# Four copies of local key and value caches, issued in the down projection by ScalarE and not in the first projections by SyncE

## The reference, cut to what matters

```
mod = silu(c) @ w_ada + b_ada                 # 6 x 1024 columns: shift, scale, gate, twice
h = x * (1 + scale1) + shift1
proj = h @ w_in                               # 1024 x 3072: qa, ka, va, qb, kb, vb, 512 columns each
... rotary, dilated window attention (A), paged differential attention (B)
mixed = concat(oa, ob) @ w_o
x = layer_norm(ALPHA * x + gate1 * mixed)
u = (x * (1 + scale2) + shift2) @ w_up        # 1024 x 5632
y = (gelu(conv(a)) * conv(g)) @ w_down        # 2816 x 1024
x = layer_norm(ALPHA * x + gate2 * y)
kk = concat([cwk, k], 1); vv = concat([cwv, v], 1)
win_k_sample, win_v_sample = kk[:, DS:], vv[:, DS:]
```

## Time and profile before

| | us |
|---|---|
| median of 3 runs | 1179.2 (1174.07 to 1181.84) |
| the profiled execution | 1176.66 |
| its span, first to last instruction | 1175.0 |
| PE busy | 1023.7 (87%) |
| DVE busy | 827.1 (70%) |
| POOL busy | 450.5 (38%) |
| ACT busy | 270.8 (23%) |

### The profile page before, as it was taken

One profiled execution on the slowest core, in us unless ns is written; L12 is line 12 of the kernel. 1 busy time (PEld: TensorE's weight loads), 2 busy tenths in 40 slices (PEclk: granted clock), 3 DMA queues, 4 the chain that ended last, 5 costly groups with the idle time before them and its releaser, 6 DMA issues.

```text
span 1175.0 us, 23900 instructions
## 1 busy us (share of the span) xinstructions
PE 1023.7 (87%) x9297; PEld 832.1 (71%) x9297; DVE 827.1 (70%) x1545; ACT 270.8 (23%) x600; POOL 450.5 (38%) x575
## 2 busy tenths in 40 slices
PE   4599989995788888888888969999999999998994
PEld 2377657673566666566676759999999999776873
DVE  1637545644886877888876784676676767999978
ACT  0300000001343433343352032323232323000001
POOL 0423223214243444434406034565566656333323
PEclk8699999998898989898998988999999999999998
DMA  8948799978899999999963151677676622414102
GB/s 299 410 157 312 269 351 365 318 246 266 289 365 368 327 337 368 349 331 331 337 253 127 42 190 47 219 255 277 248 253 250 215 73 75 155 60 147 53 2 80
DMA packets 101030, 276.54 MB, mean 235 GB/s; under 512 B 9608, under 2 KB 33174, under 8 KB 97317
## 3 DMA queue, kind: packets, MB, share of 16 engines
q1 hardware_dynamic: 85701, 223.56, 54.2%
q0 software_dynamic: 15168, 51.39, 12.6%
q10 hardware_dynamic: 48, 0.05, 0.0%
HBM read 264.60 MB, written 76.69 MB: 290 GB/s over the span
## 4 chain that ended last, share of the span: by engine, by line
PE 53%; DVE 16%; issue 15%; DMA 6%; POOL 5%; SPq 2%; POOLq 2%; ACT 1%; ACTq 0%; DVEq 0%; PEldq 0%
PE wide L1723 15%; PE wide L1724 14%; PE wide L1725 14%; DMA ring<-in_w_ada 2%; DVE ring_r L1180 2%; POOLq L480 1%; PE wide L1666 1%; POOL room L509 1%; DVE ht_r L1533 1%; DMA room<-in_w_ada 1%; DVE ring L1260 1%; POOL x_sb L509 1%; POOL x_sb L805 1%; PE wide L1807 1%; DVE ring_r L1179 1%
## 5 line engine op out<-in xcount | busy, mean ns | idle before, releaser
L828 POOL TENSOR_TENSOR ring_r<-ring,ring_r 128x1024 fp32r<-128x1024 f32 x70 | 180.8, 2592 | 232.3 <-DVE ring_r L1139 201.1
L1723 PE MATMUL wide<-x_sb_r,ring_r 128*128 128x288 f32 x704 | 211.1, 300 | 11.4 <-DVE ht_r L1162 8.4
L1724 PE MATMUL wide<-ht_r,ring_r 128*128 128x288 f32 x704 | 209.3, 297 | 0.0
L1725 PE MATMUL wide<-x_sb_r,ring_r 128*128 128x288 f32 x704 | 208.7, 297 | 0.0
L1723 PEld LDWEIGHTS wide<-x_sb_r,ring_r 128*128 128x128 f32 x704 | 133.4, 190 | 14.3 <-issue 14.3
L1260 DVE STREAM_TRANSPOSE ring<-ring 128x512 f32<-128x512 f32 x208 | 129.0, 677 | 12.0 <-DMA ring<-in_cache_k 10.3
L1725 PEld LDWEIGHTS wide<-x_sb_r,ring_r 128*128 128x128 f32 x704 | 134.2, 191 | 0.0
L1724 PEld LDWEIGHTS wide<-ht_r,ring_r 128*128 128x128 f32 x704 | 133.8, 190 | 0.0
L1723 PE MATMUL wide<-ring_r,x_sb_r 128*128 128x512 f32 (+1 forms) x208 | 87.0, 418 | 11.9 <-DVE ht_r L1162 8.7
L1725 PE MATMUL wide<-ring_r,ht_r 128*128 128x512 f32 x216 | 87.2, 404 | 0.0
L1724 PE MATMUL wide<-ring_r,x_sb_r 128*128 128x512 f32 (+1 forms) x208 | 83.7, 402 | 0.0
(11 more groups left out here) (271 smaller groups left out, 2119.4 us busy)
## 6 DMA issues: line engine op xcount, KB each, us to landing
ring<-in_cache_k SPq DMA_DIRECT2D x128, 256.0 KB
out_wks<-in_cache_win_k SPq DMA_DIRECT2D x8, 4080.0 KB, 19.5
out_wvs<-in_cache_win_v SPq DMA_DIRECT2D x8, 4080.0 KB, 19.3
ring<-in_w_up SPq DMA_DIRECT2D x22, 1024.0 KB, 7.6
room<-in_w_ada SPq DMA_DIRECT2D x8, 2048.0 KB, 9.7
ring<-in_cache_win_k SPq DMA_DIRECT2D x16, 1024.0 KB
x_sb<-in_cache_v POOLq DMA_DIRECT2D x60, 256.0 KB, 5.4
room<-in_cache_v POOLq DMA_DIRECT2D x56, 256.0 KB, 5.3
```

What stands on the lines that cost most here:

```text
L828: nc.gpsimd.tensor_tensor(rest, w, high.bitcast(F32), ALU.subtract).then_inc(wl_rest, 1)
L1723: nc.tensor.matmul(out, left[0], right[0], start=first, stop=False)
L1724: nc.tensor.matmul(out, left[0], right[1], start=False, stop=False)
L1725: return nc.tensor.matmul(out, left[1], right[0], start=False, stop=last)
```

## The change

`COPY_UNIT` keeps four entries: the copies of sequences 0 and 1, behind units 1, 8, 15 and 22. The copies of sequences 2 and 3 are issued by ScalarE in the down projection: that of keys of sequence 2 behind its third copy of convolution rows, that of values behind the eighth, and those of sequence 3 behind its last one, when 24 and when 31 gated tiles have been split. `move_window` becomes a function that takes the engine. The copies of sequences 4 to 7 stay where they were.

```diff
--- before.py
+++ after.py
@@ -61,7 +61,7 @@
 
 
 LATE_UNIT = {4: 3, 5: 6, 6: 10, 7: 13, 8: 16, 9: 20, 10: 23, 11: 26}
-COPY_UNIT = {1: (0, "k"), 4: (0, "v"), 8: (1, "k"), 11: (1, "v"), 14: (2, "k"), 18: (2, "v"), 21: (3, "k"), 24: (3, "v")}
+COPY_UNIT = {1: (0, "k"), 8: (0, "v"), 15: (1, "k"), 22: (1, "v")}
 
 
 UP0 = range(8, 12)
@@ -519,6 +519,11 @@
                         .then_inc(landed, 16)
 
 
+        def move_window(eng, i, which):
+
+            name, dst = (("cache_win_k", "wks"), ("cache_win_v", "wvs"))[which]
+            eng.dma_start(o[dst][0, i, 0:PAST - DS], a[name][0, i, DS:PAST]).then_inc(copied, 16)
+
         @block.sync
         def _(sp):
             def load_chunk(n):
@@ -580,11 +585,6 @@
                     sp.wait_ge(ada_mm, ch)
                 src = a["w_ada"][0].rearrange("(k p) n -> p k n", p=P)
                 sp.dma_start(late, src[:, :, CH * ch:CH * ch + CH]).then_inc(late_in, 16)
-
-            def move_window(i, names=(("cache_win_k", "wks"), ("cache_win_v", "wvs"))):
-                for name, dst in names:
-                    sp.dma_start(o[dst][0, i, 0:PAST - DS], a[name][0, i, DS:PAST]).then_inc(copied, 16)
-
 
             def flat(ap):
                 return ap.rearrange("t h d -> t (h d)")
@@ -631,7 +631,7 @@
                         load_late(ch + 1)
                 if n in COPY_UNIT:
                     i, which = COPY_UNIT[n]
-                    move_window(i, (("cache_win_k", "wks") if which == "k" else ("cache_win_v", "wvs"),))
+                    move_window(sp, i, "kv".index(which))
 
 
             sp.wait_ge(page_in, 16)
@@ -705,7 +705,7 @@
                 load_chunk(n)
                 if n < FIRST_LATE + 12:
                     i = n - FIRST_LATE - 4
-                    move_window(4 + i // 2, ((("cache_win_k", "wks"), ("cache_win_v", "wvs"))[i % 2],))
+                    move_window(sp, 4 + i // 2, i % 2)
             load_chunk(FIRST_LATE + 13)
             sp.wait_ge(spilled, 16 * TP)
             sp.wait_ge(spilled_last, 16)
@@ -1066,6 +1066,12 @@
                 if i >= 2:
                     act.wait_ge(conv_st[i % 2], 32 * (i // 2))
                 nc.scalar.activation(conv_out(i), bk(6 + i % 2)[0:18, :], ACT.Copy).then_inc(us_a, 1)
+                if i in (2, 7):
+                    move_window(act, 2, i // 7)
+
+            for which, z in enumerate((24, 31)):
+                act.wait_ge(g_split, z)
+                move_window(act, 3, which)
 
             def scale_norm(t):
                 rows = P if t < TP else NS
```

## The result

| | us |
|---|---|
| before, median of 8 runs | 1175.49 (1172.43 to 1181.84) |
| after, median of 8 runs | 1190.26 (1182.72 to 1196.60) |
| ratio | 1.0118, 95% interval 1.0082 to 1.0154 |
| the profiled execution of after | 1196.60 |
| its span | 1194.9 |

The change makes the kernel slower by 1.2%: 13.9 us of 1175.49 by the ratio (9.6 to 18.1 by its interval), 14.8 between the two medians. The profiled execution of after is the longest of its eight, 6.3 us over their median, so single waits are read from it and the size is read from the runs.

A forecast was written before the change was run, and what follows sets the result against it. It took TensorE's and VectorE's work to bound the kernel, with few DMA waits in the chain. 5.1 + 1.35 + 6.0 = 12.45 us on the median 1179.2 gave 1191.7, own range 1186 to 1198, wider range 1182 to 1198.

The forecast's parts named there:

- What is removed gives nothing: First projections: taking copies off SP's queue removes no wait; nothing counted.
- The old wait of 3.65: First projections: TensorE idles 3.65 us for the w_ada slice issued at 137.74; put down to 2 MB of w_in ahead.
- rival 2: First projections: without the copy of 142.54 that slice lands earlier, no new wait appears; -5.0 us, 1174.2; chance 0.05.
- The slice behind the copy: First projections: the last w_ada slice stands behind unit 22's copy, landing 5.5 us after it; TensorE waits 5.1 us.
- Slow matmuls: First projections: after that wait TensorE's 16 matmuls take 3.18 us instead of 1.83, 1.35 us more.
- The chunk beside ScalarE's copy: Down projection: w_down's fourth chunk shares the DMA engines with ScalarE's second copy; VectorE waits 6.0 us more.
- equal shares: Down projection: the load needs twice its 6.1 us while the copy lasts, 6.1 us more; taken as 6.0.
- the upper bound: Down projection: the chunk's load runs wholly behind the copy, landing at 1072.0 instead of 1064.39, 7.6 us.
- Rival 4: Down projection: long copy rows starve the w_down load, and the load behind the third copy is late; 1197, chance 0.05.
- Rivals 1 and 3: Both places: 1, only one new wait appears, 1185.7 or 1185.2, chance 0.19; 3, unseen cover for both, 1179, 0.09.

The follow-up runs named there:

- both waits taken away: Changed kernel with SP's fourth copy behind unit 24 and ScalarE's second to fourth copies behind 24, 31 and 38 split tiles; 1175.11, ratio 0.9990.
- ScalarE's second copy behind the chunk: Changed kernel with ScalarE's second copy moved behind the 24th split, the third and fourth behind the 31st and 38th; 1182.05, ratio 1.0064.
- the copy beside the load: Changed kernel with ScalarE's second copy issued behind the ninth copy of convolution rows, just behind the fourth chunk of w_down; 1193.55, ratio 1.0125.
- short rows: Changed kernel with ScalarE's second copy behind the ninth copy of convolution rows, made in two DMAs with rows of 2,040 bytes; 1186.30, ratio 1.0083.

## Why the prediction was right, and where it was wrong

The time, the sign and the mechanism held: 1190.26 against 1191.7 forecast, and two waits at the two places named. Part of the closeness is luck. The base of 1179.2 was the median of three runs, and that of eight is 3.7 lower; the sum of 12.45 lies 1.5 below the 13.9 of the ratio and 2.3 below the 14.8 between the medians. The two errors partly cancel.

- **What is removed gives nothing.** Right, and shown: with both waits taken away the kernel is at 0.9990. The old wait of 3.65 stays at 3.59, though the copy of 142.54 that stood behind its slice is gone. The slice lands after 12.7 us as before, so rival 2 falls. It goes when the slice is loaded ahead of w_in; as a copy moved in the same run, w_in alone isn't shown to be the cause.
- **The slice behind the copy, 5.1.** Measured 4.84, inside 4.5 to 5.8. The step carried the 5.5 us from the landing of a copy to that of the slice behind it to another place; there it was 245.04 to 250.65, 5.6. In the three experiments that keep this wait (ScalarE's second copy behind the chunk, the copy beside the load, short rows) it is 5.81, 5.50 and 5.32.
- **Slow matmuls, 1.35.** Mis-sized: 2.71. The step took only the 16 matmuls from the earlier trace rows, and these behind a wait of 3.65. After 4.84 the 16 took 3.60 instead of 3.18, and the five behind them lost another 0.94 at the clock of 0.50. One trace doesn't fix this term: from the timelines of the same three experiments these 21 matmuls lost 2.1, 1.7 and 2.4 us, behind the longer waits.
- **The chunk beside ScalarE's copy, 6.0.** This step failed in its mechanism, though 6.54 lies near it and within its bounds. The step was "I take 6.0, the equal shares". The engines are shared row by row, so the load ran practically behind the copy, which was the upper bound: 7.6 there, of which 0.6 goes for a copy that took 15.4 and not 16.0 us, and 0.6 for a chunk issued 6.4 and not 5.75 us behind it, which leaves 6.4. Equal shares were near by accident, because the copy and the chunk were issued 6.4 us apart. Issued together they give 11.73, where twice the load's 6.1 would give about 6.
- **The rule in the Trainium skill** ("DMA: Bandwidth & Descriptors", section "Queues, rings and completion order"), that each DMA engine takes turns between its queues a packet at a time: the trace agrees as to the turns, with 48 rows against 48. It doesn't bear out the 9 to 17 descriptors that the section has in a typical packet: here a turn was one row. The prediction drew "equal shares or a little more" from it; with rows of 65,280 and 2,048 bytes it should have drawn 32 to 1. The lengths of the rows were in the shapes of the two transfers.
- **Rival 4**, the starving load, is this mechanism; its price was not. The chunk beside the third copy, issued 0.9 us ahead of it, took 19.5 us to land (issued 1090.29, landed 1109.8) and VectorE wants it at 1115.51: still hidden, with 5.7 us to spare. **Rivals 1 and 3** fall with the two waits, each of which was shown to cost 0.6% alone.
- **Not foreseen:** ScalarE's waits of 7 to 8 us for small stores beside its own copies, about a microsecond more than it idles there anyway. They cost nothing: with both waits away the kernel stands at 0.9990 although one such wait of 7.24 us is still in it.

## What to carry to other kernels

Before a large transfer is moved to an emptier stage, look for the loads that have no slack there, and issue it right behind the landing of such a load; the busy share of the DMA engines says nothing about that, and moving two of the issues away from such loads, with the last two a step on, brought the whole 1.2% back. A queue of its own doesn't protect a load from a copy: the shares follow the lengths of the rows, so a bulk copy beside urgent traffic is cut into rows no longer than those of that traffic; here the copy itself then took 20.3 us instead of 17.0. And look for what stands ahead of a late load in its own queue: loading one slice ahead of 2 MB that were less urgent, with a copy moved along, gave the only gain found here, 0.45%.

## What the runs showed of the hardware

- In every case measured here two queues shared the DMA engines row by row, whichever was issued first: 48 rows of 65,280 bytes against 48 of 2,048 in 10.5 us, and 277 against 277 in 3 us where both were about 2 KB.
- A store of 32 KB beside a long-row copy lands about as late as a load of 2 MB: the store issued at 1029.96 held ScalarE until 1044.37, 14.4 us, where the chunk took 14.7; beside the copy issued behind the chunk ScalarE idled 11.71 us for one.
- After 4.84 us of idling TensorE worked for 5.6 us at a granted clock of 0.50 before it had 0.99, which added 2.71 us. The loss didn't grow with the wait: after 5.3 to 5.8 us of idling in three other kernels it was 1.7 to 2.4 us, and after 3.77 us in the kernel with short rows there was none, at a granted clock of 1.00.
